# An address change in a float32 transformer trunk: weight rings and arena at new offsets in SBUF

## The reference, cut to what matters

```
for i in range(DEPTH):                                   # DEPTH = 2
    h = rms_norm(x, norm_mix[i])
    mem_kv = rms_norm(mem, norm_mem[i]) @ w_mem_kv[i]    # 2048 x 1024
    ... = h @ w_in_a[j]   or   h @ w_in_b[j]             # 2048 x 2432, 2048 x 6656
    mix = swa_sink_attention(...)  or  hgrn2_chunkwise(...)
    x = x + concatenate([mix, memory_attention(...)]) @ w_o[i]           # 2048 x 2048
    gate, up = split(rms_norm(x, norm_ffn[i]) @ w_gate_up[i])            # 2048 x 11264
    x = x + (silu(gate) * up) @ w_down[i]                                # 5632 x 2048
```

## The kernel before

| tile | offset | modulo 128 |
|---|---|---|
| x_tok | 16512 | 0 |
| hT_hi, hT_lo | 32896, 49280 | 0 |
| raw, w_hi, w_lo | 65664, 82048, 98432 | 0 |
| ident | 133248 | 0 |
| arena: gT_hi, gT_lo | 138976, 184032 | 96 |
| arena: mixT_hi and _lo, memT_hi and _lo | 138976 and on, in steps of 16384 | 96 |

## Time and profile before

### The profile page before, as it was taken

The page is one execution under the profiler, slowest core; times in us unless marked ns, Lnnn a source line. Parts: engine busy times, 40 slices in busy tenths (PEclk is TensorE's granted clock), DMA queues, the critical chain, the costliest instruction groups (busy, mean ns, idle before and its releaser), DMA issues.

```text
span 2291.1 us, 29587 instructions
## 1 busy us (share of the span) xinstructions
PE 2272.7 (99%) x10710; PEld 1880.4 (82%) x10710; DVE 1271.0 (55%) x1498; ACT 1007.5 (44%) x1242; POOL 55.9 (2%) x85
## 2 busy tenths in 40 slices
PE   8999999999999999999999999999999999999999
PEld 6888888888888888888888888888888888888887
DVE  6756665555555554444556666665555555554443
ACT  5656544444444443344443434344444444443332
POOL 2101000000000000000000000000000000000000
PEclk9999999999999999999999999999999999999999
DMA  7564446666666665655554545456666666666664
GB/s 247 171 201 128 131 156 195 189 189 189 190 186 190 192 184 178 193 185 185 175 145 144 164 147 165 147 184 184 192 187 189 189 187 192 185 191 195 199 193 130
DMA packets 213277, 410.29 MB, mean 179 GB/s; under 512 B 13264, under 2 KB 13516, under 8 KB 213196
## 3 DMA queue, kind: packets, MB, share of 16 engines
q1 hardware_dynamic: 212108, 407.11, 58.8%
q10 hardware_dynamic: 1088, 2.10, 0.2%
HBM read 407.06 MB, written 2.10 MB: 179 GB/s over the span
## 4 chain that ended last, share of the span: by engine, by line
PE 92%; DVE 1%; issue 0%; ACT 0%; POOL 0%; DVEq 0%; ACTq 0%
PE unit_bank L1364 86%; PE mix_bank L1385 2%; PE mix_bank L1520 2%; PE mix_bank L1451 0%; PE mix_bank L1414 0%; DVE w_lo L833 0%; PE mix_bank L1423 0%; PE mix_bank L1505 0%; DVE tanh_q L1065 0%; PE mix_bank L1460 0%; PE mix_bank L1435 0%; PE mix_bank L1549 0%; PE mix_bank L1547 0%; PE mix_bank L1540 0%; PE mix_bank L1530 0%
## 5 line engine op out<-in xcount | busy, mean ns | idle before, releaser
L833 DVE TENSOR_TENSOR w_lo<-raw,w_hi 128x1024 fp32r<-128x1024 f32 x768 | 936.9, 1225 | 826.9 <-ACT w_hi L488 817.2
L488 ACT ACTIVATE w_hi<-raw 128x1024 fp32r<-128x1024 f32 x768 | 810.5, 1060 | 973.0 <-PE unit_bank L1364 947.7
L1364 PE MATMUL unit_bank<-w_hi,hT_hi 128*128 128x512 f32 (+1 forms) x1984 | 778.0, 392 | 0.0
L1364 PE MATMUL unit_bank<-w_hi,hT_lo 128*128 128x512 f32 (+1 forms) x1984 | 771.2, 389 | 0.0
L1364 PE MATMUL unit_bank<-w_lo,hT_hi 128*128 128x512 f32 (+1 forms) x1984 | 770.2, 388 | 0.0
L1364 PEld LDWEIGHTS unit_bank<-w_hi,hT_lo 128*128 128x128 f32 x1984 | 372.4, 188 | 77.1
L1364 PEld LDWEIGHTS unit_bank<-w_lo,hT_hi 128*128 128x128 f32 x1984 | 372.7, 188 | 74.0
L1364 PEld LDWEIGHTS unit_bank<-w_hi,hT_hi 128*128 128x128 f32 x1984 | 372.6, 188 | 74.1 <-issue 0.3
L1364 PE MATMUL unit_bank<-w_hi,gT_hi 128*128 128x512 f32 x704 | 279.5, 397 | 0.0
L1364 PE MATMUL unit_bank<-w_hi,gT_lo 128*128 128x512 f32 x704 | 279.1, 396 | 0.0
L1364 PE MATMUL unit_bank<-w_lo,gT_hi 128*128 128x512 f32 x704 | 279.0, 396 | 0.0
(11 more groups left out here) (227 smaller groups left out, 1114.7 us busy)
## 6 DMA issues: line engine op xcount, KB each, us to landing
raw<-in_w_gate_up SPq DMA_DIRECT2D x352, 512.0 KB, 4.2
raw<-in_w_down SPq DMA_DIRECT2D x176, 512.0 KB, 4.5
raw<-in_w_in_b SPq DMA_DIRECT2D x104, 512.0 KB, 4.3
raw<-in_w_o SPq DMA_DIRECT2D x64, 512.0 KB, 4.0
raw<-in_w_in_a SPq DMA_DIRECT2D x40, 512.0 KB, 3.9
raw<-in_w_mem_kv SPq DMA_DIRECT2D x32, 512.0 KB, 4.5
mem_tok<-in_mem SPq DMA_DIRECT2D x4, 512.0 KB, 8.8
x_tok<-in_x SPq DMA_DIRECT2D x4, 512.0 KB, 8.5
```

What stands on the lines that cost most here:

```text
L488: act.activation(w_hi[:, s, :, :], raw[:, s, :, :], ACT.Copy).then_inc(sems["hi_ready"], 1)
L833: dve.tensor_tensor(w_lo[:, s, :, :], raw[:, s, :, :], w_hi[:, s, :, :].bitcast(F32), ALU.subtract).then_inc(sems["lo_ready"], 1)
L1364: ins = pe.matmul(unit_bank[2 * pair + tile][:, 0:cols], a, b[:, s, j, 0:cols], start=opens and n == 0 and j == 0 and m == 0, stop=closes ...
```

## The change

The small tiles that were behind the large ones go in part to the front, `x_tok` is set to a multiple of 2048 bytes, the rows of `w_hi` get 16 more bytes each (4 unused elements), `w_lo` and the arena are set to multiples of 128.

```
-        def keep(name, shape, dtype=F32):
+        def keep(name, shape, dtype=F32, line=32):
             size = int(np.prod(shape)) * 4
-            place[0] = -(-place[0] // 32) * 32
+            place[0] = -(-place[0] // line) * line
...
-        x_tok = keep("x_tok", [TILES, D])
+        ident = keep("ident", [P])
+        q_gain = keep("q_gain", [HD_A])
...
+        x_tok = keep("x_tok", [TILES, D], line=2048)
         hT = (keep("hT_hi", [KT, SEQ], F32R), keep("hT_lo", [KT, SEQ], F32R))
         raw = keep("raw", [RING, 2, COLS])
-        w_hi = keep("w_hi", [RING, 2, COLS], F32R)
-        w_lo = keep("w_lo", [RING, 2, COLS], F32R)
+        w_hi = keep("w_hi", [RING, 2, COLS + 4], F32R)
+        w_lo = keep("w_lo", [RING, 2, COLS], F32R, line=128)
...
-        arena = -(-place[0] // 32) * 32
+        arena = -(-place[0] // 128) * 128
...
-                act.activation(w_hi[:, s, :, :], raw[:, s, :, :], ACT.Copy).then_inc(sems["hi_ready"], 1)
+                act.activation(w_hi[:, s, :, 0:COLS], raw[:, s, :, :], ACT.Copy).then_inc(sems["hi_ready"], 1)
...
-                dve.tensor_tensor(w_lo[:, s, :, :], raw[:, s, :, :], w_hi[:, s, :, :].bitcast(F32),
+                dve.tensor_tensor(w_lo[:, s, :, :], raw[:, s, :, :], w_hi[:, s, :, 0:COLS].bitcast(F32),
                                   ALU.subtract).then_inc(sems["lo_ready"], 1)
```

More of the change, by code:

```diff
@@ L161, in keep @@
             return t
-        x_tok = keep("x_tok", [TILES, D])
+        ident = keep("ident", [P])
+        q_gain = keep("q_gain", [HD_A])
+        k_gain = keep("k_gain", [HD_A])
+        g_gain = keep("g_gain", [HD_B])
+        cos = keep("cos", [TILES, ROT])
+        sin = keep("sin", [TILES, ROT])
+        ang = keep("ang", [TILES, ROT])
+        turn = keep("turn", [TILES, ROT])
+        freq = keep("freq", [ROT])
+        pos_int = keep("pos_int", [TILES], I32)
+        sum_sq = keep("sum_sq", [TILES, BLOCKS])
+        sum_two = keep("sum_two", [TILES, 2])
+        x_tok = keep("x_tok", [TILES, D], line=2048)
         hT = (keep("hT_hi", [KT, SEQ], F32R), keep("hT_lo", [KT, SEQ], F32R))
         raw = keep("raw", [RING, 2, COLS])
-        w_hi = keep("w_hi", [RING, 2, COLS], F32R)
-        w_lo = keep("w_lo", [RING, 2, COLS], F32R)
+        w_hi = keep("w_hi", [RING, 2, COLS + 4], F32R)
+        w_lo = keep("w_lo", [RING, 2, COLS], F32R, line=128)
         kmT_b = keep("kmT_b", [4, N_MEM])
@@ L172, in trunk @@
         squares = keep("squares", [COLS])
-        ident = keep("ident", [P])
         level_mask = keep("level_mask", [LEVELS, P // 2])
         columns = keep("columns", [ROWS])
-        q_gain = keep("q_gain", [HD_A])
-        k_gain = keep("k_gain", [HD_A])
-        g_gain = keep("g_gain", [HD_B])
         sink = keep("sink", [KV_A * GROUP_A])
         minus_sink = keep("minus_sink", [KV_A * GROUP_A])
[L181 to L186, removed]
         lb_work = keep("lb_work", [4, HEADS_B])
@@ L189, in trunk @@
         decay_now = keep("decay_now", [3, 4])
-        sum_sq = keep("sum_sq", [TILES, BLOCKS])
-        sum_two = keep("sum_two", [TILES, 2])
         mem_sum_sq = keep("mem_sum_sq", [TILES, BLOCKS])
@@ L236, in trunk @@
         mixT = (take("mixT_hi", [KT, SEQ], F32R), take("mixT_lo", [KT, SEQ], F32R))
-        take = arena_map(2 * half, 2 * half + 3 * half)
+        take = arena_map(2 * half, 5 * half)
         q_a = take("q_a", [TILES, COLS])
```

## The result

The changed kernel takes 2313.51 us (median of 4 runs, 2312.39 to 2313.67) against 2292.79 for the kernel before (median of 4): a ratio of 1.0089, whose 95% interval, 1.0071 to 1.0106, leaves out 1. It is slower by 20.7 us, 0.9%. 2312 was forecast.

The account below looks back on a forecast made before the run. The prediction took the distance between starts of TensorE's weight matmuls as the bound; from 2292.8 us, arena gain and padding loss together added 20, giving 2313, stated as 2312. Full range 2244 to 2342, the forecast's own 2298 to 2340.

Parts of the forecast that it names:

- What bounds the kernel: TensorE's stream of 9,216 weight-product matmuls: time is the distance between starts, and nothing feeding TensorE is late.
- (a): Arena moved from 96 to 0 modulo 128: its 3264 matmuls fall from 234.3 to 226.9 ns, 24.2 us gained.
- (b): Padded w_hi rows make the moving start jump, so weight products cannot settle: mean 231.7 ns a matmul.
- the column count: Lower bound for matmuls on padded w_hi rows: 213.3 ns, the time of 512 columns alone.
- twice the excess: Upper bound for matmuls on padded w_hi rows: gT's 7.4 ns over the settled 226.9, doubled, giving 242.
- (c): Sum over 9120 matmuls of 512 columns: mean 229.5 to 231.7 ns, 20 us more; hT loses 28, arena wins 8.5.
- (d): ScalarE's copy and VectorE's subtraction on spread w_hi rows: at most 10% longer each, hidden by waits, taken as nothing.
- Inert moving rows: Rival: the moving row's address does not matter in weight products, all run at 226.9 ns, 2269 us; chance 0.15.
- Rotation: Rival: each matmul start waits for its place in a 128-byte rotation, 224.2 ns a matmul, 2245 us; chance 0.21.
- dead time: Some 2.5 ns between matmuls, taken from 256-column matmuls on L1414, below which a jump must wait another rotation.
- Slow by itself: Rival: moving rows off a 64- or 128-byte border are slow, up to 242 ns, 2366 us; chance 0.10 (over 2340).
- signs to watch: In the new chain: hT pieces at 44.3 to 44.8 us, gT at 231 to 232 ns, starts that no longer repeat.

Follow-up runs that it names:

- align_only: Changed kernel without the 16-byte padding of w_hi rows, so hT, both rings and arena begin at 0 modulo 128: 2271.08 us.
- ht32_ar64: Changed kernel without padding, hT at 32, both rings at 128 and arena at 192 modulo 256: 2326.41 us.
- whi_at_32: Changed kernel without padding, all of w_hi at 32 modulo 256, hT at 0, w_lo and arena at 128: 2310.10 us.
- lo_at_64: Changed kernel without padding, w_lo at 64 modulo 256, hT and w_hi at 0, arena at 128: 2311.83 us.
- rings_at_128: Changed kernel without padding, w_hi, w_lo and arena at 128 modulo 256, hT at 0: 2302.58 us.
- all_at_32: Changed kernel without padding, hT, w_hi, w_lo and arena all at 32 modulo 256: 2270.28 us.
- ar224: Changed kernel without padding, hT and both rings at 0 modulo 256, arena at 224: 2290.42 us.
- pad_arena96: Changed kernel, padding kept, with only the arena set back to 96 modulo 128: 2314.24 us.
- htlo_at_64: Changed kernel without padding, hT_lo at 64 modulo 256, hT_hi at 0, both rings and arena at 128: 2305.77 us.
- rings_at_32: Changed kernel without padding, w_hi and w_lo at 32 modulo 256, hT and arena at 0: 2325.49 us.

## Why the prediction was right

*What bounds the kernel.* Right, and it is what made the rest possible: the time is the distance between starts times their number, and it moved with that alone.

*(a), the arena.* Right: 24.2 us forecast for it alone, 22 measured (align_only). Added up in the two traces from start to start, weight products with gT take 15.95 us less than before, with mixT 5.00 and with memT 2.26, so 23.2 together; 2.2 us come back between the last product of a stretch with memT or mixT and the other matmul that follows.

*(b), the padding.* The size was right: 231.7 ns forecast as the mean, 231.9 with hT and 231.8 with gT measured. The choice that carried it was to take rows of this kernel in which the stream was out of step, 231.7 after other matmuls, and not the column count or twice the excess. That it fits to 0.2 ns is in part luck. All slow pieces of the study lie between 231.1 and 234.3 ns, and by the sum of (c) any mean between these makes 2307 to 2337 us, all inside the forecast's 2298 to 2340. Nor do the two values that made up the mean hold by kind: with hT the next start comes 232.0 ns after a w_lo matmul and 231.9 after a w_hi one, where 231 and 232 were taken. The reason was right in part: the fast rate needs all moving rows and stationary blocks at one place. It was wrong in three things. The period is 256 bytes and not 128, so that row r = 2 against hT (32) was not gT's case before (160); 233.3 and 234.3 are near enough that the sum did not notice. The fast rate is not the only one that repeats: ht32_ar64 repeats exactly at 233.3 with gT, at a distance of 192. And the forecast blamed the jump from one start to the next, but the loss comes without any jump: constant distances other than 0 cost 232.4 to 234.3, a jumping moving operand 231.1 to 232.9.

Does each matmul simply pay for its own distance? In three stretches all distances are ones that were also measured by themselves (the table at the end). In whi_at_32 hT has hi matmuls at 32 (233.3) and lo ones at 128 (232.4), which would make 233.0, and takes 231.1. In lo_at_64 gT has hi at 128 and lo at 192, which would make 232.7, and takes 241.30 / 1044 = 231.1. Only the third nearly fits: in whi_at_32 gT has hi at 160 and lo at 0, which would make 231.8, and takes 232.2. And in rings_at_128 the same distance gives 232.4 in most pieces and 233.3 in every fourth. So the rate belongs to the sequence, not to the single matmul. What in the chip makes it is not settled by these runs.

*(c), the sum.* 28 lost and 8.5 won forecast; 28.1 and 8.4 found, added up over the traces.

*(d), the splits.* Right: 1060 and 1225 ns as before. The waits of the two are longer by 19.0 and 15.7 us, since the stream that they wait for is longer, and TensorE's is 5.0 us as before.

*The rivals.* Inert moving rows: whi_at_32 would be 2269 and is 2310. Rotation: it would be 2225. (The dead time of that rival, 2.5 ns, is 2.9 by its own rows, 216.2 over 213.3; a jump of two places still exceeds it, so its sum stands.) Slow by itself: all_at_32 would be over 2300 and is 2270. Of the signs to watch, one was wrong: I said that the starts would no longer repeat; they do, with the ring.

The Trainium skill (SBUF — State Buffer, Who interferes with whom) gives TensorE two independent read ports and says that it never waits on anyone. By that rule the distance of two operands' addresses would cost nothing. These runs do not agree: with gT, 226.7 ns a matmul in align_only and 233.3 in ar224, at the same granted clock, shapes and order. Whether anything waits at a port they do not show.

## What to carry to other kernels

When TensorE is the bound and its stream has no waits, divide pieces of the chain by their matmuls, tensor by tensor, and compare: a few ns between groups of the same shape can be an address. Put the rows of the moving operand and the blocks of the stationary one at the same place modulo 256 bytes, all of them (measured here for float32r rows of 512 columns), and check that with the offsets that the allocator really gave, since padding one ring shifts the next. If one spread of rows breaks the relation, aligning the rest need not bring anything: in pad_arena96 and the changed kernel it made no difference.

## What the runs showed of the hardware that was not expected

Float32r matmuls of 512 columns, each with its own weight load of 128 columns, at the full granted clock:

| moving minus stationary, modulo 256 | ns from start to start | where |
|---|---|---|
| 0 | 226.7 to 226.9 | before (hT), align_only, all_at_32, ar224 (hT), rings_at_128 and htlo_at_64 (gT) |
| 32 | 233.3 | rings_at_32 (both), ar224 (gT) |
| 96 | 233.3 | ht32_ar64 (hT) |
| 128 | 232.4, every fourth piece 233.3 | rings_at_128 (hT) |
| 160 | 234.3 | before (gT) |
| 192 | 233.3 | ht32_ar64 (gT) |

The table is of the pieces' lengths divided by their counts. Distance 0 is the only fast one of those tried; 64, 224 and odd multiples of 16 bytes were not tried as a constant distance. No arrangement came under 226.7, though the columns alone take 213.3.
